# Feed-forward products that read their moving weight columns from last to first and write PSUM in the same reversed order

## The chip, the core and the metric

The kernel runs on one core of one Trainium2 chip. The metric is device time in microseconds (us), the median of several runs. [...]

## The reference, cut to what matters

The reference is one decoder layer on 256 tokens of width 2048, in float32. A mixer (an input projection, three kinds of attention, gated branches, an output projection) is followed by the part that this change touches:

```python
def swiglu(h, w_gate, w_up, w_down):
    return (jax.nn.silu(h @ w_gate) * (h @ w_up)) @ w_down
...
        h = rms_norm(x, norm_ffn[layer])
        x = x + swiglu(h, w_gate[layer], w_up[layer], w_down[layer])
    return rms_norm(x, norm_final)
```

`w_gate` and `w_up` are 2048 x 5632, `w_down` is 5632 x 2048.

## The kernel before

**The products.** Float32 is multiplied in parts. Each factor is split into a high part (type float32r, rounded, called `hi`) and the rest (`lo`), and every product is three matmuls: hi·hi, hi·lo and lo·hi (L638 to L640; L877 to L880 in the up products). Tokens are the stationary operand, a block of 128 features x 128 tokens; weights are the moving operand, 128 features x 256 columns in the feed-forward part. One matmul writes 128 tokens x 256 columns of a PSUM bank (512 float32 columns, so half a bank), and the three matmuls of a product write the same half.

**Units.** The weights come through a ring of four slots in units of 2 x 128 features x 512 columns. For each unit SyncE issues one transfer into `raw_ring`, ScalarE rounds it into `weight_hi_ring` (L1039), VectorE subtracts to get `weight_lo_ring` (L1269), and TensorE uses both: a plain unit is 24 matmuls (2 blocks x 2 token tiles x 2 column halves x 3). The slot is free when the last of them has counted `unit_used` up. The list `FFN` fixes the order of the units: 88 of gate, 88 of up and 88 of down, in two halves of the 5632 columns.

**Two forms of product.** Gate and down units run through `products`. The up units run through `up_unit` and its helper `into`; 55 of the 88 up units do with seven block products instead of eight (21 matmuls, not 24), for which VectorE and ScalarE prepare sums of weights (`weight_sums_hi`, `weight_sums_lo`) and sums of token blocks (`h_sums`). Its other 33 units have 24.

**Where things lie.** The weight rings start 128 bytes into a line of 512 bytes and the stationary tiles 192 bytes into one (`MOVING, STATIONARY = 128, 192`). Each row of 256 moving columns is 1024 bytes without a gap, read upwards.

**After the products.** VectorE and ScalarE read the banks in plain order (silu L1078, up rows L1321 to L1325, the residual add L1348), and TensorE transposes the 512 new columns of activations (L627) for the down products. After the last down unit comes a final norm and the store.

Of the kernel before, what the change touches and what calls it, by code (L numbers as in the profile page):

```python
# [21 lines left out]
TT = 2  # L22
# [3 lines left out]
W = 512  # L26
# [26 lines left out]
UK = 2  # L53
RING = 4
UPC = KD // UK
# [5 lines left out]
Q4 = W // 2  # L61
# [169 lines left out]
def build_layer(nc, x_in, norm_mix, w_in, sinks, pe_k, w1_k, w2_k, pe_v, w1_v, w2_v,  # L231
                w_br_a, w_br_b, w_br_c, w_out, norm_ffn, w_gate, w_up, w_down, norm_final, out):
    ctx = ExitStack()
    with ctx:
# [3 lines left out]
        def at(name, shape, offset, dt=F32):  # L238
            return nc.alloc_sbuf_tensor_at(name, [P] + shape, dt, offset=offset)

        def place(name, shape, dt=F32):
            n = 4
            for s in shape:
                n *= s
            n = (n + 31) // 32 * 32
            t = at(name, shape, top[0], dt)
            top[0] += n
            assert top[0] <= nc.sbuf_top, name
            return t

        raw = place("raw_ring", [RING, UK, W])
        whi = place("weight_hi_ring", [RING, UK, W], F32R)
        wlo = place("weight_lo_ring", [RING, UK, W], F32R)
# [46 lines left out]
        h2T_hi = at("h2T_hi", [KD, S], mid, F32R)  # L300
        h2T_lo = at("h2T_lo", [KD, S], mid + 4 * KD * S, F32R)
        span = [low]

        def follow_on(name, shape, dt=F32):
            n = 4
            for d in shape:
                n *= d
            t = at(name, shape, span[0], dt)
            span[0] += n
            assert span[0] <= mid, name  # L310
            return t

        actT_hi = follow_on("actT_hi", [KH, S], F32R)
        actT_lo = follow_on("actT_lo", [KH, S], F32R)
# [9 lines left out]
        ext_hi = at("weight_sums_hi", [2, 3, Q4], ext_at, F32R)  # L324
        ext_lo = at("weight_sums_lo", [2, 3, Q4], ext_at + 2 * 3 * 4 * Q4, F32R)
# [28 lines left out]
        bank = [ctx.enter_context(nc.psum_tensor(f"bank{i}", [P, W], F32)) for i in range(8)]  # L354

        def sem(name):
            return ctx.enter_context(nc.semaphore(name))
# [4 lines left out]
        unit_used = sem("unit_used")  # L362
# [262 lines left out]
        def _(pe):  # L625
            def transpose(dst, src, n=P):
                return pe.transpose(dst, src, ident[0:n, 0:n])  # L627

            def products(slot, lhs, pair, first, last, k0, width=W, tiles=tuple(range(TT))):

                l_hi, l_lo = lhs
                parts = [(0, Q4), (Q4, W)] if width == W else [(0, width)]
                for k, t, (a, b) in [(k, t, part) for k in range(UK) for t in tiles for part in parts]:
                    dst = bank[2 * pair + t][:, a:b]
                    x_hi, x_lo = (m[:, k0 + k, t * P:(t + 1) * P] for m in (l_hi, l_lo))
                    w_hi, w_lo = (m[:, slot, k, a:b] for m in (whi, wlo))
                    opening = first and k == 0 and a == 0
                    pe.matmul(dst, x_hi, w_hi, start=opening, stop=False, skip_group_check=True)  # L638
                    pe.matmul(dst, x_hi, w_lo, start=False, stop=False, skip_group_check=True)  # L639
                    m = pe.matmul(dst, x_lo, w_hi, start=False, stop=last and k == UK - 1, skip_group_check=True)  # L640
                return m
# [230 lines left out]
            def into(i, b, q, lhs, rhs, stop):  # L872

                l_hi, l_lo = lhs
                r_hi, r_lo = rhs
                dst = bank[b][:, q * Q4:(q + 1) * Q4]
                pe.matmul(dst, l_hi, r_hi, start=(i, b) not in opened, stop=False, skip_group_check=True)  # L877
                opened.add((i, b))
                pe.matmul(dst, l_hi, r_lo, start=False, stop=False, skip_group_check=True)  # L879
                return pe.matmul(dst, l_lo, r_hi, start=False, stop=stop, skip_group_check=True)  # L880

            def quarters(u, k, c):

                return tuple(m[:, u % RING, k, c * Q4:(c + 1) * Q4] for m in (whi, wlo))

            def up_unit(u, i, j):

                def block(k, t):
                    return tuple(m[:, UK * j + k, t * P:(t + 1) * P] for m in (h2T_hi, h2T_lo))

                stop = j == UPC - 1
                if not is_seven(u):
                    for k in range(UK):
                        into(i, 3, 0, block(k, 0), quarters(u, k, 0), stop)
                        into(i, 2, 0, block(k, 0), quarters(u, k, 1), stop)
                        into(i, 2, 1, block(k, 1), quarters(u, k, 0), stop)
                        m = into(i, 3, 1, block(k, 1), quarters(u, k, 1), stop)
                    return m
                n, e = SEVEN.index(j), N_SEVEN[u] % 2
                if i == 0:  # L900
                    pe.wait_ge(h_sum_lo, n + 1)

                def total(r):
                    return tuple(m[:, n, r, :] for m in (h2S_hi, h2S_lo))

                def extra(r):
                    return tuple(m[:, e, r, :] for m in (ext_hi, ext_lo))

                into(i, 6, 0, block(0, 0), quarters(u, 0, 0), True)
                into(i, 3, 0, block(1, 0), quarters(u, 1, 0), False)  # L910
                into(i, 2, 0, total(3), quarters(u, 1, 1), False)
                into(i, 6, 1, total(1), quarters(u, 0, 1), True)
                into(i, 7, 0, total(0), extra(0), True)
                into(i, 7, 1, total(2), extra(1), True)
                return into(i, 2, 1, block(1, 1), extra(2), False)

            def ffn_unit(u):

                what, i, j = FFN[u - U_FFN]
                if what == "gate":  # L920
                    if j == 0 and i == 0:
                        pair_free(Q_FFN)
                    elif j == 0 and half_of(i) != half_of(i - 1):
                        pe.wait_ge(added, TT * (NC_D - 1))
                    elif j == 0:
                        pe.wait_ge(silu_ready, i)
                    if i == 0:
                        pe.wait_ge(t_lo, 2 * UPC + j + 1)
                    pe.wait_ge(lo_ready, u + 1)
                    products(u % RING, (h2T_hi, h2T_lo), 0, j == 0, j == UPC - 1, UK * j).then_inc(unit_used, 1)  # L930
                elif what == "up":
                    if j == 0 and i == 0:
                        pair_free(Q_FFN + 1)
                        pe.wait_ge(squares, 2 * TT * NC_D)
                    elif j == 0:
                        pe.wait_ge(up_emptied, i)
                        if half_of(i) != half_of(i - 1):
                            pe.wait_ge(added, TT * NC_D)
                    pe.wait_ge(lo_ready, u + 1)
                    up_unit(u, i, j).then_inc(unit_used, 1)  # L940
                else:
                    h, c = i
                    n, done = KD_H[h], TT * (NC_D * h + c - 1)
                    if j == 0 and c == 0:
                        pe.wait_ge(silu_ready, HALVES[h][1])
                    elif j == 0 and c == 1:
                        pe.wait_ge(up_emptied, HALVES[h][1])
                    elif j == 0:
                        pe.wait_ge(added, done)
                    if c == 0:  # L950
                        pe.wait_ge(aT_lo, 2 * (HALVES[h][0] + j // 2 + 1))
                    if i == LAST_DOWN and j >= n - RING:
                        return
                    pe.wait_ge(lo_ready, u + 1)
                    products(u % RING, (actT_hi, actT_lo), c % 2, j == 0, j == n - 1, UK * j).then_inc(unit_used, 1)

            def last_units():

                n = KD_H[1]
                for t in range(TT):  # L960
                    for j in range(n - RING, n):
                        u = AT["down", LAST_DOWN, j]
                        if t == 0:
                            pe.wait_ge(lo_ready, u + 1)
                        m = products(u % RING, (actT_hi, actT_lo), LAST_DOWN[1] % 2, False, j == n - 1, UK * j,
                                     tiles=(t,))
                        if t == TT - 1:
                            m.then_inc(unit_used, 1)
                    if t == 0:
                        m.then_inc(tile0_full, 1)  # L970
# [21 lines left out]
            for u in range(UPC):  # L992
# [3 lines left out]
                if u == 3:  # L996
                    pe.wait_ge(rows_ready, 48)
                    pe.wait_ge(gains_ready, 1)
                    for a in range(1, 4):
                        m = transpose(bank[2][:, KD * a:KD * (a + 1)], rows[0:KD, a, :], KD)  # L1000
# [674 lines left out]
```

## Time and profile before

| | |
|---|---|
| median of 3 runs | 1381.56 us (1380.27 to 1384.85) |
| span of the profiled execution, first to last instruction | 1378.3 us |
| TensorE busy | 1364.8 us, 99% of the span |
| TensorE weight loads busy | 1332.1 us, 97% |
| VectorE busy | 922.5 us, 67% |
| ScalarE busy | 702.5 us, 51% |
| mean granted TensorE clock | 0.999 |
| transfers | 261.08 MB, mean 189 GB/s |

The span is of one profiled execution; of its own total time the profile gives only this span, so everything outside it is taken from the distance to the median, 3.3 us. "Busy" of TensorE is the union of matmuls that overlap one another in the pipeline: a single one lasts some 0.28 us from its start to its modelled end, yet another starts every 0.11 us. Its rate is therefore read from the starts, or from how many matmuls a stretch of known length holds.

### The profile page before, as it was taken

The page shows a single profiled execution, that of the slowest core. Times are in us where ns is not written, and L with a number is a line of the kernel's source. Part 1 is how long each engine was busy: PE and PEld are TensorE (multiplying, and loading weights), DVE is VectorE, ACT ScalarE, POOL GpSimd, SP SyncE. Part 2 cuts the span into 40 slices and gives each one's busy share as a digit, 9 for nine tenths or more (in the row PEclk, how much of TensorE's full clock was granted, in tenths as well). Part 3 has the DMA queues.
Part 4 walks back from the last instruction along what each step waited for, and adds up shares of the span by engine and source line. Part 5 has one row for each costly group of instructions (what it writes and reads, how often), then busy time and mean ns, then how long its engine had stood idle before and what let it go on. Part 6 is the DMA issues. An engine that isn't in the chain of part 4 may idle for free.

```text
span 1378.3 us, 26427 instructions
## 1 busy us (share of the span) xinstructions
PE 1364.8 (99%) x11280; PEld 1332.1 (97%) x11280; DVE 922.5 (67%) x1189; ACT 702.5 (51%) x912; POOL 46.2 (3%) x70
## 2 busy tenths in 40 slices
PE   8999999999999999999999999999999999999997
PEld 8999999999999999999999999999999999999997
DVE  6455557667654657666788788875446788887554
ACT  7333356656545654465654555454334455545444
POOL 4000010000000110000000000000000000000111
PEclk9999999999999999999999999999999999999999
DMA  7777755455565767546556756566556665666653
GB/s 255 245 217 217 212 148 154 140 151 141 152 192 163 198 204 221 179 163 200 165 181 198 219 171 196 185 208 210 195 195 181 191 211 172 196 194 231 210 195 123
DMA packets 135264, 261.08 MB, mean 189 GB/s; under 512 B 8448, under 2 KB 25408, under 8 KB 134768
## 3 DMA queue, kind: packets, MB, share of 16 engines
q1 hardware_dynamic: 133328, 251.89, 59.8%
q0 software_dynamic: 1792, 7.57, 1.5%
q8 instruction: 86, 1.41, 0.4%
q14 instruction: 26, 0.21, 0.0%
q10 hardware_dynamic: 32, 0.01, 0.0%
HBM read 257.33 MB, written 2.10 MB: 188 GB/s over the span
## 4 chain that ended last, share of the span: by engine, by line
PE 89%; DVE 8%; ACT 1%; issue 1%; ACTq 0%; POOL 0%; DVEq 0%; POOLq 0%
PE bank L638 24%; PE bank L639 23%; PE bank L640 23%; PE bank L877 5%; PE bank L880 4%; PE bank L879 4%; PE bank L627 2%; DVE weight_lo_ring L1269 2%; DVE weight_sums_lo L1289 1%; DVE weight_sums L1278 1%; PE bank L776 1%; DVE act_rows L1329 1%; ACT weight_hi_ring L1039 1%; PE bank L687 1%; DVE raw_ring L1280 1%
## 5 line engine op out<-in xcount | busy, mean ns | idle before, releaser
L1269 DVE TENSOR_TENSOR weight_lo_ring<-raw_ring,weight_hi_ring 128x1024 fp32r<-128x1024 f32 (+2 forms) x480 | 581.0, 1220 | 317.0 <-ACT weight_hi_ring L1039 263.4
L1039 ACT ACTIVATE weight_hi_ring<-raw_ring 128x1024 fp32r<-128x1024 f32 (+2 forms) x432 | 449.1, 1052 | 348.6 <-PE bank L640 281.1
L638 PE MATMUL bank<-weight_hi_ring,hT_hi 128*128 128x256 f32 (+2 forms) x1280 | 384.5, 300 | 0.8 <-DVE weight_lo_ring L1269 0.8
L639 PE MATMUL bank<-weight_lo_ring,hT_hi 128*128 128x256 f32 (+2 forms) x1280 | 378.0, 295 | 0.0
L640 PE MATMUL bank<-weight_hi_ring,hT_lo 128*128 128x256 f32 (+2 forms) x1280 | 377.8, 295 | 0.0
L638 PEld LDWEIGHTS bank<-weight_hi_ring,hT_hi 128*128 128x128 f32 x1280 | 241.1, 188 | 12.5 <-issue 7.5
L639 PEld LDWEIGHTS bank<-weight_lo_ring,hT_hi 128*128 128x128 f32 x1280 | 240.5, 188 | 4.5
L640 PEld LDWEIGHTS bank<-weight_hi_ring,hT_lo 128*128 128x128 f32 x1280 | 240.4, 188 | 4.7
L638 PE MATMUL bank<-weight_hi_ring,h2T_hi 128*128 128x256 f32 x704 | 196.3, 279 | 2.2 <-DVE weight_lo_ring L1269 2.1
L640 PE MATMUL bank<-weight_hi_ring,h2T_lo 128*128 128x256 f32 x704 | 195.3, 277 | 0.0
L639 PE MATMUL bank<-weight_lo_ring,h2T_hi 128*128 128x256 f32 x704 | 195.2, 277 | 0.0
L638 PE MATMUL bank<-weight_hi_ring,actT_hi 128*128 128x256 f32 x704 | 194.5, 276 | 0.0
L639 PE MATMUL bank<-weight_lo_ring,actT_hi 128*128 128x256 f32 x704 | 194.3, 276 | 0.0
L640 PE MATMUL bank<-weight_hi_ring,actT_lo 128*128 128x256 f32 x704 | 194.3, 276 | 0.0
L638 PEld LDWEIGHTS bank<-weight_hi_ring,h2T_hi 128*128 128x128 f32 x704 | 132.2, 188 | 4.0 <-DVE weight_lo_ring L1269 3.3
L640 PEld LDWEIGHTS bank<-weight_hi_ring,h2T_lo 128*128 128x128 f32 x704 | 132.5, 188 | 0.0
L639 PEld LDWEIGHTS bank<-weight_lo_ring,h2T_hi 128*128 128x128 f32 x704 | 132.5, 188 | 0.0
L639 PEld LDWEIGHTS bank<-weight_lo_ring,actT_hi 128*128 128x128 f32 x704 | 132.2, 188 | 0.0
L638 PEld LDWEIGHTS bank<-weight_hi_ring,actT_hi 128*128 128x128 f32 x704 | 132.2, 188 | 0.0
L640 PEld LDWEIGHTS bank<-weight_hi_ring,actT_lo 128*128 128x128 f32 x704 | 132.2, 188 | 0.0
L1036 ACT ACTIVATE weight_sums_hi<-weight_sums 128x768 fp32r<-128x768 f32 x55 | 46.6, 847 | 127.8 <-DVE weight_sums L1281 61.4
L877 PE MATMUL bank<-weight_hi_ring,h2T_hi 128*128 128x256 f32 x374 | 105.1, 281 | 0.0
(238 smaller groups left out, 1883.2 us busy)
## 6 DMA issues: line engine op xcount, KB each, us to landing
raw_ring<-in_w_in SPq DMA_DIRECT2D x96, 512.0 KB, 3.6
raw_ring<-in_w_gate SPq DMA_DIRECT2D x88, 512.0 KB, 4.3
raw_ring<-in_w_up SPq DMA_DIRECT2D x88, 512.0 KB, 4.2
raw_ring<-in_w_down SPq DMA_DIRECT2D x88, 512.0 KB, 4.1
raw_ring<-in_w_in SPq DMA_DIRECT2D x56, 452.0 KB, 3.7
raw_ring<-in_w_out SPq DMA_DIRECT2D x32, 512.0 KB, 3.9
raw_ring<-in_w_br_c SPq DMA_DIRECT2D x16, 256.0 KB, 3.9
raw_ring<-in_w_br_a SPq DMA_DIRECT2D x16, 256.0 KB, 6.7
```

The source lines that it names most:

```text
L627: return pe.transpose(dst, src, ident[0:n, 0:n])
L638: pe.matmul(dst, x_hi, w_hi, start=opening, stop=False, skip_group_check=True)
L639: pe.matmul(dst, x_hi, w_lo, start=False, stop=False, skip_group_check=True)
L640: m = pe.matmul(dst, x_lo, w_hi, start=False, stop=last and k == UK - 1, skip_group_check=True)
L687: pe.matmul(dst[:, S:2 * S], v[0], pT[:, i % 2, h, 0:S], start=True, stop=False)
L776: m = pe.matmul(bank[4 + h][:, P * t:P * (2 * t + 1)], qT[half, pr, P * t:P * (t + 1)], keys[half, 0:P * (t + 1)], start=True, stop=True)
L877: pe.matmul(dst, l_hi, r_hi, start=(i, b) not in opened, stop=False, skip_group_check=True)
L879: pe.matmul(dst, l_hi, r_lo, start=False, stop=False, skip_group_check=True)
L880: return pe.matmul(dst, l_lo, r_hi, start=False, stop=stop, skip_group_check=True)
L1036: act.activation(ext_hi[:, n % 2, :, :], t_sum[:, :, :], ACT.Copy)
L1039: act.activation(whi[:, s, :, 0:width(u)], raw[:, s, :, 0:width(u)], ACT.Copy).then_inc(hi_ready, 1)
L1269: dve.tensor_tensor(lo, w, hi.bitcast(F32), ALU.subtract).then_inc(lo_ready, 1)
```

## The change

In the feed-forward part each matmul's moving operand is read from its last column to its first, and its PSUM output is addressed from the last column to the first as well. The numbers land where they did before. Addresses of the tiles, the order of the instructions, their count (10383 rows on TensorE in both programs), the waits and the transfers stay the same, as do the products of the mixer, the stationary operands, the transposes and everything that VectorE and ScalarE do.

```diff
-            def products(slot, lhs, pair, first, last, k0, width=W, tiles=tuple(range(TT))):
+            def products(slot, lhs, pair, first, last, k0, width=W, tiles=tuple(range(TT)), back=False):
...
                     dst = bank[2 * pair + t][:, a:b]
+                    if back:
+                        dst = dst[:, ::-1]
                     x_hi, x_lo = (m[:, k0 + k, t * P:(t + 1) * P] for m in (l_hi, l_lo))
                     w_hi, w_lo = (m[:, slot, k, a:b] for m in (whi, wlo))
+                    if back:
+                        w_hi, w_lo = w_hi[:, ::-1], w_lo[:, ::-1]
...
-                dst = bank[b][:, q * Q4:(q + 1) * Q4]
+                dst = bank[b][:, q * Q4:(q + 1) * Q4][:, ::-1]
...
-                return tuple(m[:, u % RING, k, c * Q4:(c + 1) * Q4] for m in (whi, wlo))
+                return tuple(m[:, u % RING, k, c * Q4:(c + 1) * Q4][:, ::-1] for m in (whi, wlo))
...
-                    return tuple(m[:, e, r, :] for m in (ext_hi, ext_lo))
+                    return tuple(m[:, e, r, ::-1] for m in (ext_hi, ext_lo))
```

The gate call, the down call and the one for the last four down units (`last_units`) each get `back=True`. The mixer's calls of `products` don't.

## Rows read from the trace of the kernel before

**Rows 1.** The page: span, and busy time of each engine.
```profile
span 1378.3 us, 26427 instructions
PE 1364.8 (99%) x11280; PEld 1332.1 (97%) x11280; DVE 922.5 (67%) x1189; ACT 702.5 (51%) x912; POOL 46.2 (3%) x70
```

**Rows 2.** The page: granted clock, tenths of full speed, in 40 slices.
```profile
PEclk9999999999999999999999999999999999999999
```

**Rows 3.** The page: the chain that ended last, shares by engine.
```profile
PE 89%; DVE 8%; ACT 1%; issue 1%; ACTq 0%; POOL 0%; DVEq 0%; POOLq 0%
```

**Rows 4.** TensorE's groups, shapes apart: busy us, mean ns of one.
```profile
L638 PE MATMUL bank<-weight_hi_ring,h2T_hi 128*128 128x256 f32 x704 | 196.3, 279 | 2.2 <-DVE weight_lo_ring L1269 2.1
...
L638 PE MATMUL bank<-weight_hi_ring,actT_hi 128*128 128x256 f32 x704 | 194.5, 276 | 0.0
...
L877 PE MATMUL bank<-weight_hi_ring,h2T_hi 128*128 128x256 f32 x374 | 105.1, 281 | 0.0
...
L877 PE MATMUL bank<-weight_hi_ring,h_sums_hi 128*128 128x256 f32 x110 | 30.5, 277 | 0.0
...
L877 PE MATMUL bank<-weight_sums_hi,h_sums_hi 128*128 128x256 f32 x110 | 30.5, 277 | 0.0
...
L877 PE MATMUL bank<-weight_sums_hi,h2T_hi 128*128 128x256 f32 x55 | 15.2, 277 | 0.0
```

**Rows 5.** TensorE in three stretches: length, busy, matmuls, clock, DMA.
```profile
680.00:740.00 60.00, 60.00 (x512) 1.00 0.66 198
...
940.00:1080.00 140.00, 140.00 (x1238) 1.00 0.60 192
40.00:140.00 100.00, 100.00 (x486) 1.00 0.74 223
```

**Rows 6.** TensorE in order of time, in a down chunk.
```profile
939.74 0.28 PE L640 MATMUL bank<-weight_hi_ring,actT_lo 128*128 128x256 f32 x1
939.85 0.28 PE L638 MATMUL bank<-weight_hi_ring,actT_hi 128*128 128x256 f32 x1
939.97 0.28 PE L639 MATMUL bank<-weight_lo_ring,actT_hi 128*128 128x256 f32 x1
940.08 0.28 PE L640 MATMUL bank<-weight_hi_ring,actT_lo 128*128 128x256 f32 x1
```

**Rows 7.** TensorE in order of time, the 452-column products of the mixer.
```profile
99.68 0.37 PE L640 MATMUL bank<-weight_hi_ring,hT_lo 128*128 128x452 f32 x1
```

**Rows 8.** The chain by time: start, us, what; eight passes each.
```profile
318.03 1.73 PE bank L802 x8
...
547.72 0.87 PE bank L627 x8
```

**Rows 9.** TensorE in order of time, a read with a step of two.
```profile
172.97 0.69 PE L725 MATMUL bank<-identity,proj 128*64 128x64 f32 x16
173.59 0.39 PE L638 MATMUL bank<-weight_hi_ring,hT_hi 128*128 128x256 f32 x1
```

**Rows 10.** All engines, the feed-forward stretch: busy and instructions of each.
```profile
660.00:1378.00 718.00, 708.31 (x6187) 705.89 (x6185) 516.73 (x617) 352.48 (x402) 11.14 (x7) 1.00 0.61 192
```

**Rows 11.** Waits of TensorE and VectorE, 655 to 1371: total, times, longest.
```profile
PE bank L638 <- DVE weight_lo_ring L1269: 2.1, 8, 0.6
...
DVE weight_lo_ring L1269 <- ACT weight_hi_ring L1039: 126.8, 93, 2.0
```

**Rows 12.** Groups, shapes apart: the 256-column float32 passes, the transposes.
```profile
L802 PE MATMUL bank<-probs_T,vc_block_diagonal 128*128 128x256 f32 x8 | 1.9, 378 | 0.0
...
L627 PE MATMUL bank<-identity,act_rows 128*128 128x128 f32 x88 | 11.4, 272 | 0.0
```

More of the change, by code:

```diff
@@ L929, in ffn_unit @@
                     pe.wait_ge(lo_ready, u + 1)
-                    products(u % RING, (h2T_hi, h2T_lo), 0, j == 0, j == UPC - 1, UK * j).then_inc(unit_used, 1)
+                    products(u % RING, (h2T_hi, h2T_lo), 0, j == 0, j == UPC - 1, UK * j, back=True).then_inc(unit_used, 1)
                 elif what == "up":
@@ L954, in ffn_unit @@
                     pe.wait_ge(lo_ready, u + 1)
-                    products(u % RING, (actT_hi, actT_lo), c % 2, j == 0, j == n - 1, UK * j).then_inc(unit_used, 1)
+                    products(u % RING, (actT_hi, actT_lo), c % 2, j == 0, j == n - 1, UK * j,
+                             back=True).then_inc(unit_used, 1)
             def last_units():
@@ L965, in last_units @@
                         m = products(u % RING, (actT_hi, actT_lo), LAST_DOWN[1] % 2, False, j == n - 1, UK * j,
-                                     tiles=(t,))
+                                     tiles=(t,), back=True)
                         if t == TT - 1:
```

## The prediction, made before the changed kernel had run

> **What bounds the kernel now.** [...] From 660 to 1378 us it is busy 708.3 of 718.0 us, VectorE 516.7, ScalarE 352.5, DMA 61% [rows 10]. Its waits name only 2.1 us on VectorE's low parts, in 8 places. VectorE does wait, for ScalarE, 126.8 us in 93 places [rows 11], but this is time that it has to spare. So TensorE's own rate sets the end.
>
> That rate comes from how close together the matmuls start. In a down chunk they start at 939.74, 939.85, 939.97, 940.08 [rows 6], 0.113 us apart. A long stretch gives it more exactly: 140 us hold 1238 matmuls [rows 5]; one lasts 277 ns [rows 4], so those that began up to 0.277 us before the stretch are counted too: (140 + 0.277)/1238 = 113.3 ns. [...]
>
> **The change part by part.** How many matmuls: gate and down, each 704 on three lines, are 6 x 704 = 4224. The up products are three lines each of 374, 110, 110 and 55, which is 3 x 649 = 1947 [rows 4]. Together 6171. At 113.3 ns they are 699 us, just over half of the span. Each ns per matmul is worth 6.2 us, or 0.45% of the whole. This is the lever, and nothing hides it.
>
> Nothing else moves. No instruction is added, removed or reordered; transfers, waits, the stationary reads, the 88 transposes [rows 12] and the banks' readers see the same addresses. An edit that leaves TensorE's rate alone is thus free without needing any cover, and one that slows it has none. If it gets slower, the others have more room: VectorE's waits [rows 11] grow, and nothing new is late. If it gets faster, VectorE at 516.7 of 718 us [rows 10] stays below it on average.
>
> The unknown price is that of reading 256 float32r columns downwards and of writing them downwards. No row shows a step of minus one, so I bound it. From below: transposes pass 128 columns in 0.87/8 us = 109 ns [rows 8]. [...]
>
> [...] I take no change: 113.3 ns.
>
> [...]
>
> The sum: 1378.3 us + 6171 x 0 = 1378.3 us of span, and with the 3.3 us between this span and the median, 1381.6 us. I keep 1381.6.
>
> **The rivals.**
> First, half rate. [...] Then 6171 x (216 - 113.3) = 634 us are added, 2015 us. [...] Chance 0.20. [...]
>
> Second, a worse meeting of streams. The same matmul runs at 113.3 or 117.7 ns in stretches that differ in nothing that its own operands show [rows 5], so the rate depends on how the moving stream and the next weight load (97% busy, [rows 1]) fall together. Reversing one and not the other changes it. With all matmuls at 117.7 ns: 6171 x 4.4 = +27 us, less about 3 us for some 90 us which are already there, +24, 1406 us. With 122 ns, no head start: 6171 x 8.6 = +53, 1435 us. Chance 0.18.
>
> Third, a better meeting, by the same argument. [...] At 109 ns: 6171 x 4.3 = -27 us, 1355 us; half of it, 1368. [...] Against it: the offsets 128 and 192 are part of how the streams meet now, and with the other direction nothing says that they'd meet better. Chance 0.17.
>
> That the change does nothing, because hardware or compiler sees the two reversals cancel, gives the same 1381.6 and belongs to my forecast. Chance of that and of a harmless reversal together: 0.45.
>
> **How the numbers follow.** The prediction is that of the likeliest case, 1381.6 us. Alone its range is 1377.5 to 1385.7, that is 0.3%, about what a measurement of this kernel can tell from no change (the three runs lie 0.3% apart). The better meeting reaches down to 1355 and the worse one up to 1435; half rate, with 2 in 10, stays outside. Range 1354 to 1436. Faster by over 0.3%: 0.17. Within: 0.45. Slower: 0.18 + 0.20 = 0.38.
>
> **What would show it.** The down chunk shows it best, since nothing else runs on TensorE in it: 1238 matmuls in 140 us if I am right, some 1191 at 117.7 ns, 650 at 216 ns, 1287 at 109 ns. The mixer's 452-column stretch must hold 486 in 100 us in any case, and the feed-forward part must begin within 1 us of where it does now. If it is half rate, VectorE's waits for ScalarE and for TensorE's banks grow by hundreds of us and DMA falls to a third of the time. If the time changes while the starts stay 113.3 ns apart, my argument is wrong altogether, since then the cost lies in a wait that I don't see. [...]

## The result and the profile after

The changed kernel takes 1399.83 us (median of 4 runs, 1398.67 to 1400.41). The kernel before, beside it, takes 1381.92 us (1380.27 to 1384.85). The ratio is 1.0121, 95% interval [1.0098, 1.0143]. It is slower, by 18 us. I had given "no change" as the likeliest and 0.18 to a worse meeting of streams at 117.7 ns and 1406 us, and that is near what came.

The page of the kernel after: span, busy time of each engine, granted clock, and the shares of the chain that ended last.

```profile
span 1397.8 us, 26427 instructions
...
PE 1387.0 (99%) x11280; PEld 1356.1 (97%) x11280; DVE 922.4 (66%) x1189; ACT 702.8 (50%) x912; POOL 45.4 (3%) x70
...
PEclk9999999999999999999999999999999999999999
...
PE 99%; DMA 0%; DVE 0%; ACT 0%; SPq 0%; ACTq 0%; issue 0%
```

Clock and instruction counts are those of [rows 1, 2]. TensorE has 22 us more of busy time, VectorE and ScalarE have the same as before. The chain had 8% on VectorE in [rows 3] and has none now; 99% of it lie on TensorE.

TensorE in stretches of the kernel after: length, busy, matmuls, clock, DMA. Beside [rows 5] they tell nearly everything.

```profile
680.00:740.00 60.00, 60.00 (x507) 1.00 0.64 193
940.00:1080.00 140.00, 140.00 (x1191) 1.00 0.58 185
...
40.00:140.00 100.00, 100.00 (x486) 1.00 0.73 222
```

The down chunk holds 1191 matmuls where it held 1238: (140 + 0.277)/1191 = 117.8 ns. The mixer's 452-column stretch, which the change doesn't touch, still holds 486. In order of time, in the same down chunk as [rows 6]:

```profile
939.87 0.28 PE L644 MATMUL bank<-weight_hi_ring,actT_lo 128*128 128x256 f32 x1
939.99 0.28 PE L642 MATMUL bank<-weight_hi_ring,actT_hi 128*128 128x256 f32 x1
940.11 0.28 PE L643 MATMUL bank<-weight_lo_ring,actT_hi 128*128 128x256 f32 x1
940.22 0.28 PE L644 MATMUL bank<-weight_hi_ring,actT_lo 128*128 128x256 f32 x1
940.34 0.28 PE L642 MATMUL bank<-weight_hi_ring,actT_hi 128*128 128x256 f32 x1
```

The steps aren't equal any more. In nanoseconds the starts come 115, 118 or 119, and 120 apart, again and again (sum 353.3 ns for three matmuls), where the kernel before has 113 to 114 each time. TensorE runs in a fixed rhythm, and in a slower one. The stretch from 680 us shows yet another rhythm: 507 matmuls are 118.9 ns on average, because from 672 to 712 us the starts lie 120.0 apart and later 117.8. TensorE in its two parts:

```profile
680.00:712.00 32.00, 32.00 (x269) 1.00 0.65 198
714.00:755.00 41.00, 41.00 (x351) 1.00 0.66 204
```

**The account.** From the first to the last feed-forward matmul the trace of before has 719.8 us, that of after 738.8, +18.9. Both traces have the same instructions in the same order, so each distance between two starts can be set beside its counterpart. 6224 of them are under 150 ns in both: 708.4 us before and 732.0 after, +23.6. The other 42, where TensorE of the kernel before waits or passes to or from transposes, have 11.4 us before and 6.8 after, -4.7; 23 of them are under 150 ns now. So the slower pace costs 23.6 us, and 4.7 come back, because TensorE now reaches the places later at which it used to wait for VectorE (2.1 us in 8 places before [rows 11], none after). Most of this lies at the ends of the up chunks: before, a product starts at 807.94 us and the next only at 808.43, on a `weight_lo_ring` that VectorE finished late. After, no such gap follows that up chunk.

### The profile page after: what moved, and what is told of

Read it like the earlier page. It is cut to its first block, busy times and chain, and to the rows that moved or that the text cites. A ratio compares the mean times of both kernels' runs of the same rounds, so it can differ in the third digit from the quotient of the medians.

```text
span 1397.8 us, 26427 instructions
## 1 busy us (share of the span) xinstructions
PE 1387.0 (99%) x11280; PEld 1356.1 (97%) x11280; DVE 922.4 (66%) x1189; ACT 702.8 (50%) x912; POOL 45.4 (3%) x70
## 4 chain that ended last, share of the span: by engine, by line
PE 99%; DMA 0%; DVE 0%; ACT 0%; SPq 0%; ACTq 0%; issue 0%
PE bank L642 26%; PE bank L644 26%; PE bank L643 26%; PE bank L884 5%; PE bank L881 5%; PE bank L883 5%; PE bank L627 2%; PE bank L780 1%; PE bank L691 1%; DMA x<-in_x 0%; PE bank L740 0%; PE bank L692 0%; PE bank L828 0%; PE bank L820 0%; PE bank L806 0%; PE bank L834 0%
## 5 line engine op out<-in xcount | busy, mean ns | idle before, releaser
L642 PEld LDWEIGHTS bank<-weight_hi_ring,hT_hi 128*128 128x128 f32 x1280 | 241.3, 189 | 11.4 <-issue 6.5
L644 PE MATMUL bank<-weight_hi_ring,actT_lo 128*128 128x256 f32 x704 | 198.5, 282 | 0.0
L644 PE MATMUL bank<-weight_hi_ring,h2T_lo 128*128 128x256 f32 x704 | 198.4, 282 | 0.0
L642 PE MATMUL bank<-weight_hi_ring,actT_hi 128*128 128x256 f32 x704 | 197.7, 281 | 0.0
L643 PE MATMUL bank<-weight_lo_ring,actT_hi 128*128 128x256 f32 x704 | 197.4, 280 | 0.0
```

## The experiments

In the expectations "theory 1" is that the downward moving read costs the time, "theory 2" that the downward PSUM write does. Each group of runs had the kernel before beside it. Its medians were 1388.4 us (e1, e2), 1386.2 (o1 to o3), 1383.8 (o4), 1385.5 (o5) and 1382.4 (o6).

### Which of the two reversals

e1 reads backwards and writes upwards:

```diff
-                    if back:
-                        dst = dst[:, ::-1]
...
-                dst = bank[b][:, q * Q4:(q + 1) * Q4][:, ::-1]
+                dst = bank[b][:, q * Q4:(q + 1) * Q4]
```

> The moving columns of the feed-forward products are read from last to first, PSUM is written upwards; the output's columns therefore come out in another order within each half bank. If the cost sits in the moving read (theory 1: the downward moving read meets the next weight load worse), the time is that of the changed kernel, about 1400 us, and 140 us of the down chunk hold some 1191 matmuls (117.8 ns from start to start). If it sits in the downward PSUM write (theory 2), the time is about 1382 us and the same 140 us hold some 1238 (113.3 ns).

e2 writes backwards and reads upwards:

```diff
-                    if back:
-                        w_hi, w_lo = w_hi[:, ::-1], w_lo[:, ::-1]
...
-                return tuple(m[:, u % RING, k, c * Q4:(c + 1) * Q4][:, ::-1] for m in (whi, wlo))
+                return tuple(m[:, u % RING, k, c * Q4:(c + 1) * Q4] for m in (whi, wlo))
...
-                    return tuple(m[:, e, r, ::-1] for m in (ext_hi, ext_lo))
+                    return tuple(m[:, e, r, :] for m in (ext_hi, ext_lo))
```

> The moving columns are read upwards as before, PSUM is written from last column to first, so the columns come out in another order within each half bank. Theory 1 (the moving read) expects about 1382 us and 113.3 ns from start to start, theory 2 (the PSUM write) about 1400 us and 117.8 ns. If both streams contribute, both single reversals lie between 1382 and 1400 us.

Measured: e1 1400.04 us, ratio 1.0103 [1.0076, 1.0131]; e2 1387.41 us, ratio 0.9993 [0.9967, 1.0019]. TensorE in the stretches of e1, read backwards:

```profile
680.00:740.00 60.00, 60.00 (x507) 1.00 0.63 193
940.00:1080.00 140.00, 140.00 (x1191) 1.00 0.58 185
```

And of e2, written backwards:

```profile
680.00:740.00 60.00, 59.77 (x526) 1.00 0.65 202
940.00:1080.00 140.00, 140.00 (x1237) 1.00 0.60 190
```

The read alone gives the changed kernel, to the matmul; the write alone gives the one before. Theory 2 is out. A PSUM bank written from last column to first costs nothing here: 1237 matmuls in 140 us of the down chunk against 1238, and a ratio of 0.9993.

### Is it direction, or how two streams meet? A table of blocks

m1 is a kernel of its own, in which TensorE runs the pattern of a unit (hi·hi, hi·lo, lo·hi over two blocks, two token tiles and two halves) with offsets and directions from a list:

```
CONFIGS: (moving offset, stationary offset, columns, read back, write back)
(128, 192, 256, False, False), (128, 192, 256, False, True), (128, 192, 256, True, False), (128, 192, 256, True, True), ...
```

> Not the layer: one kernel that only runs blocks of the same float32r matmuls on TensorE (48 of 256 columns per block, four transposes between blocks), and computes none of the reference. Blocks: four combinations of read and write direction at the offsets of the layer kernel (moving 128, stationary 192 bytes into a line of 512), each twice; then all 64 pairs of offsets in steps of 64 bytes upwards, and the same 64 downwards; then 128, 256, 384, 452 and 512 columns in both directions. If the pace depends on how the moving read and the weight load meet, it changes with the pair of offsets, differently for the two directions: 113.3 ns at 128/192 upwards, 117.8 ns downwards, and among the 64 downward pairs some are at 113.3 or below. If direction has a price of its own, all 64 downward pairs are at 117.8 ns or above. If offsets play no part, each direction has one pace throughout.

The pace of a block is the mean distance between its starts once the first are left out, in which it settles: eight here, ten in m2, eleven in m3 and m4, three in the blocks of twelve of m3. With another number left out most means move by some tenths of a ns. In ns, for some pairs of offsets (moving/stationary):

| offsets | upwards | downwards |
|---|---|---|
| 128/192 (4 blocks each) | 113.3 in all | 120.0 in 3, 117.8 in 1 |
| 0/0 | 120.0 | 118.4 |
| 0/64 | 113.3 | 120.0 |
| 64/64 | 120.0 | 118.4 |
| all 64 pairs | 113.3 to 120.0 | 118.2 to 120.1 |

So offsets count in both directions, but only upward blocks reach 113.3 ns. At the 16 pairs whose two offsets are equal modulo 256 bytes downward is the faster one (118.2 to 118.4 ns against 120.0). Downwards everything repeats after 256 bytes; upwards it does for all but 8 of the 64 pairs, of which 4 have 113.3 or 117.8 ns where their partners have the other. It is the relation of the two operands that counts: in m1 and m2, whose offsets go in steps of 64 and 32 bytes, every upward block at 113.3 has offsets that differ by 64 modulo 128, and none of the 320 upward blocks with another difference gets below 116.4. (At offsets of odd 16 bytes, in m3 and m4, this no longer holds: 48/192 reaches 113.3.) Widths are the other surprise. TensorE in m1, two stretches with 452 columns (up, down) and two with 512 (up, down):

```profile
875.00:879.00 4.00, 4.00 (x21) 1.00 0.00 0
908.20:912.20 4.00, 4.00 (x21) 1.00 0.00 0
880.50:885.00 4.50, 4.50 (x21) 1.00 0.00 0
914.00:918.50 4.50, 4.50 (x21) 1.00 0.00 0
```

The same number fits either way: the blocks give 206.7 and 206.8 ns, 233.5 and 233.2.

### Does the start of a block decide?

The four blocks that read up and write down or the reverse had 117.8 ns (both that only wrote downwards, and one that only read downwards) or 120.0, although e2, which only writes downwards, shows 113.3 in the layer. So one pair of offsets may have more than one rhythm. m2 starts each block at other moments, and narrows the stationary operand.

> Again only blocks of float32r matmuls, none of the layer (24 of 256 columns per block, after four transposes and, in some blocks, one float32 matmul of 16 to 128 columns that shifts the moment at which the block starts). 64 pairs of offsets in steps of 32 bytes upwards and 16 downwards, six starts each; then stationary blocks of 128, 96, 64 and 32 columns in both directions; then only one or two of the three matmuls of a product read downwards. If the pace comes from how the moving read and the weight load meet, the same pair can settle at 113.3 or 117.8 ns depending on the start when read upwards, no start brings a downward pair to 113.3, and with a weight load of 32 columns both directions have the same pace, nearer to 109 ns. If the downward read itself is slow, 32 columns leave the two directions as far apart as 128.

Upwards at 128/192: nine blocks, six at 113.3 and three at 117.8. Every upward pair of m2 that reached 113.3 also had blocks at 117.8, by the start alone. The upward slow rhythm isn't the downward one: its steps are 117 to 119 ns, not 115, 118 and 120, though three of them sum to the same 353.3. Downwards at 128/192: nine blocks, 117.5 to 117.8 in eight, 120.0 in one; no downward block of any pair is below 117.5. With only one or two of a product's three matmuls read downwards it was 117.6 to 117.9, in 18 blocks of 18: one reversed read takes the fast rhythm from all three. My expectation on narrow stationary blocks failed: with 32 columns the trace has 108 ns for a weight load in place of 188, and downwards the pace was still 118.2 to 118.5, upwards 113.4, 116.5 and 113.4. The rhythm isn't made by the length of the weight load alone.

The layer shows the two upward rhythms too. In the kernel before the starts lie 117.8 ns apart from 650.4 us on, 113.3 after the transposes at 659.6, 117.8 again after a wait at 667.8, and 113.3 from the transposes at 757.4 to the end, apart from some 3 us after each later wait. Each change comes at an interruption, though not every interruption brings one. TensorE in the kernel before, ahead of the change at 757.4 us and behind it:

```profile
714.00:756.00 42.00, 42.00 (x359) 1.00 0.62 190
770.00:806.00 36.00, 36.00 (x320) 1.00 0.66 204
```

### Do the offsets work in the layer too?

o1 is the kernel before, o2 the changed kernel, both with `MOVING, STATIONARY = 0, 0`; o3 is the changed kernel with `0, 64`.

> The kernel before with both offsets at 0 (rings and stationary tiles each begin a line of 512 bytes). The table has 120.0 ns for this pair upwards. If its blocks carry over to the layer, 9819 matmuls of 256 columns (feed-forward and mixer) cost 6.7 ns more each, +66 us: about 1448 us. If placement is nothing in the layer, 1382 to 1390.

> The changed kernel with both offsets at 0. The table has 118.4 ns downwards and 120.0 upwards for this pair. If the cost of reversing is a matter of the meeting, its sign turns here: the feed-forward part is faster than that of the upward kernel with the same offsets by 6171 x 1.6 ns = 10 us, about 1438 us. If reading downwards has a price of its own, it is again some 18 us slower than that kernel.

> The changed kernel with offsets 0 and 64. Table: upwards 113.3 (as at 128/192), downwards 120.0 in place of 117.8 to 120. The mixer keeps its pace, and the feed-forward part has 120.0 ns in the down chunk: 6171 x 2.2 ns more than the changed kernel, about 1413 us. If the offsets don't matter for downward reads, 1400.

Measured: o1 1431.64 us, ratio 1.0332 [1.0306, 1.0359]; o2 1421.44 us, 1.0260 [1.0233, 1.0286]; o3 1400.06 us, 1.0100 [1.0075, 1.0126]. The down chunk of o1, read upwards:

```profile
940.00:1080.00 140.00, 140.00 (x1170) 1.00 0.56 187
```

The down chunk of o2, read downwards:

```profile
940.00:1080.00 140.00, 140.00 (x1186) 1.00 0.58 189
```

1170 matmuls are 119.9 ns, 1186 are 118.3; the table said 120.0 and 118.4. With these offsets the reversed kernel is the faster one, by 10.2 us, as expected to the microsecond. So there is no fixed price of reading downwards: its sign turns with placement. The absolute times I had 17 us too high: 6.7 ns per matmul was counted against 113.3, but the mixer's 256-column matmuls average 114.4 ns in the kernel before, some 90 us of its feed-forward part run at 117.8, and the waits shrank by 5 us. o3 refutes one entry: its down chunk has 1191 matmuls, 117.8 ns, not the 120.0 of the first table. m2 had five of six starts near 117.8 for this pair, so the first table's single block was the rarer rhythm.

### Widths, load length, and a shift of the low parts

> Blocks of float32r matmuls only, none of the layer. Three questions. (1) Widths of 128 to 512 columns in both directions: the first table had the same pace up and down at 384, 452 and 512 columns, so I expect that direction costs something only around 256 columns, where one weight load per matmul is just hidden. (2) Stationary blocks of 64 and 32 columns at eight moving offsets: if the meeting is with the weight load, the offset matters less the shorter the load, and with 32 columns the pace is nearly flat over the offsets in both directions; if the moving read collides with something of its own, it depends on the offset as before. (3) The low parts of the moving or of the stationary operand start 32 to 224 bytes later than the high parts: if two successive moving reads collide, the first shift changes the pace and the second doesn't; if moving read and weight load collide, both do. Lastly odd 16-byte offsets.

In ns at 128/192, three starts each:

| columns | upwards | downwards |
|---|---|---|
| 128 to 224 | 111.5 to 111.8 | 111.7 to 111.8 |
| 256 | 113.3, 117.8, 113.3 | 117.8 |
| 288 | 133.0 to 133.4 | 131.6 |
| 320, 352 | 146.6 to 146.9, 160.0 | 146.6 to 146.8, 160.0 |
| 384 | 173.4 to 176.6 | 176.0 to 176.4 |
| 416 | 186.6 to 186.8 | 190.0 |
| 448 | 201.9 to 202.5 | 204.4 to 206.6 |
| 480 | 215.4 to 216.4 | 220.0 |
| 512 | 233.2 to 233.4 | 233.2 to 233.4 |

"Only around 256" was too simple: up to 224 columns there is a floor of 111.7 ns which direction doesn't touch, and above it direction is worth -1.8 to +4.6 ns, now one way, now the other. With 64 or 32 stationary columns upward blocks still reach 113.3 at some moving offsets and not at others, and no downward one is below 117.8, so the second of these expectations (flat with a short load) is wrong. Shifting the low moving part by any of seven distances loses 113.3 upwards, and so do six of seven shifts of the low stationary part. By the third expectation that speaks for a meeting of moving read and weight load, but it doesn't rule out that two moving reads meet as well. The one shift that keeps 113.3, in three of three starts, is that of the low stationary part by 128 bytes.

o4 turns the mixer's products too:

```diff
-                m = products(u % RING, lhs, q % 2, j == 0, j == n - 1, UK * j, width)
+                m = products(u % RING, lhs, q % 2, j == 0, j == n - 1, UK * j, width, back=True)
...
-                                 UK * j, WQ).then_inc(unit_used, 1)
+                                 UK * j, WQ, back=True).then_inc(unit_used, 1)
```

> The changed kernel with the mixer's products read and written backwards as well. By the theory that the price hangs on the width: the 452-column stretch keeps 486 matmuls in 100 us, the mixer's 3648 products of 256 columns cost some 3.4 ns more (117.8 in place of their mean of 114.4), +12 us over the changed kernel, some of it absorbed by waits: 1408 to 1413 us. If a downward read costs per column, the 672 products of 452 columns get 1.76 x 4.4 ns each too, +5 us more, and the stretch holds 468.

Measured: 1412.68 us, ratio 1.0206 [1.0165, 1.0246]. TensorE in o4, the down chunk and the 452-column stretch:

```profile
940.00:1080.00 140.00, 140.00 (x1192) 1.00 0.57 185
...
40.00:140.00 100.00, 100.00 (x486) 1.00 0.73 222
```

The 452-column products are read downwards at no cost, and the mixer's of 256 columns go from a mean of 114.4 to 117.9 ns. The first feed-forward matmul starts at 664.1 us in place of 650.9. Price per column is out; the price hangs on the rhythm at this width.

### A placement with one rhythm

m4 gives 16 further starts to the candidates.

> Blocks of upward float32r matmuls, none of the layer: 16 combinations of how much later the low parts of the moving and of the stationary operand start (0 to 192 bytes), eight moving offsets, two starts each; then 16 different starts for each of six pairs of offsets, and 16 for the downward read at 128/192. In the table before, the low stationary part 128 bytes later gave 113.3 ns in 3 of 3 starts, the present placement in 2 of 3. If that placement has only the fast state, all 16 starts give 113.3; if the 3 of 3 were luck, some of them give 117.8, as I expect of the present one. Downward, none of 16 starts is below 117.5.

| moving, stationary, low part later by | direction | pace in ns (blocks) |
|---|---|---|
| 128, 192, 0 (both kernels) | up | 113.3 (6), 117.8 (12) |
| 128, 192, 128 | up | 113.3 (18 of 18) |
| 0, 192, 128 | up | 113.3 (9), 118.8 to 118.9 (9) |
| 192, 192, 128 | up | 118.8 to 119.7 (18) |
| 48, 192, 0 | up | 113.3 (15), 113.8 (1) |
| 208, 192, 0 | up | 113.3 (7), 118.4 to 118.8 (9) |
| 128, 192, 0 | down | 117.8 (15), 120.0 (1) |

TensorE in m4, the start of a block with the low part 128 bytes later. It comes in with steps of 0.12 us and finds the fast rhythm by itself: the last step shown is 0.11, and those behind it are 113 or 114 ns. (At 48/192 it takes ten steps or so; with only the first eight left out its means were 113.3 to 114.7.)

```profile
943.81 0.28 PE L465 MATMUL bank<-moving_lo,stationary_hi 128*128 128x256 f32 x1
943.93 0.28 PE L465 MATMUL bank<-moving_hi,stationary_lo 128*128 128x256 f32 x1
944.05 0.28 PE L465 MATMUL bank<-moving_hi,stationary_hi 128*128 128x256 f32 x1
944.17 0.28 PE L465 MATMUL bank<-moving_lo,stationary_hi 128*128 128x256 f32 x1
944.29 0.28 PE L465 MATMUL bank<-moving_hi,stationary_lo 128*128 128x256 f32 x1
944.41 0.28 PE L465 MATMUL bank<-moving_hi,stationary_hi 128*128 128x256 f32 x1
944.52 0.28 PE L465 MATMUL bank<-moving_lo,stationary_hi 128*128 128x256 f32 x1
```

o5 puts that placement into the kernel before, o6 into the changed one. `LO = 128` is added ahead of the five low stationary tiles (`h_sb` and `h_sum` move by as much):

```diff
+        top[0] += LO
         hT_lo = place("hT_lo", [KD, S], F32R)
...
-        h2T_lo = at("h2T_lo", [KD, S], mid + 4 * KD * S, F32R)
+        h2T_lo = at("h2T_lo", [KD, S], mid + 4 * KD * S + LO, F32R)
...
+        span[0] += LO
         actT_lo = follow_on("actT_lo", [KH, S], F32R)
```

> The kernel before (upwards), with the low part of every stationary operand placed 128 bytes further into its line. If this placement has only the fast state, every run lies at about 1378 to 1380 us, since 6171 matmuls keep 113.3 ns and the mixer's 3648 gain some 1 ns each, partly lost in waits; the kernel before scatters from 1380 to 1394. If the single runs of the kernel before scatter for another reason than the two states, this one scatters as much, around 1386.

> The changed kernel (downwards) with the same new placement, low stationary parts 128 bytes further. The table has 118.5, 117.8 and 118.7 ns for it downwards, against 113.3 in 18 of 18 blocks upwards. If the placement helps only where the fast state exists, this kernel gains nothing in the feed-forward part: 739 us from its first to its last matmul (118.5 ns would make it 743), 1391 to 1192 matmuls being ruled out in favour of some 1191 to 1184 in 140 us of the down chunk, and 1396 to 1402 us in all, some 22 us above the upward kernel with the same placement. If the placement cures the downward read too, 1377.

Measured: o5 1376.96 us (1376.19 to 1378.39, 5 runs), ratio 0.9940 [0.9926, 0.9953], faster than both kernels. o6 1400.58 us (1399.90 to 1401.03), ratio 1.0139 [1.0118, 1.0160]. TensorE in o5:

```profile
680.00:740.00 60.00, 59.78 (x526) 1.00 0.68 204
940.00:1080.00 140.00, 140.00 (x1238) 1.00 0.60 190
...
40.00:140.00 100.00, 100.00 (x491) 1.00 0.74 227
```

TensorE in o6:

```profile
680.00:740.00 60.00, 60.00 (x510) 1.00 0.66 202
940.00:1080.00 140.00, 140.00 (x1184) 1.00 0.58 183
```

In o5 the stretch from 680 us, which held 512 matmuls in [rows 5], holds 526. So it does in e2, with the old placement and another entry. The feed-forward part of o5 is as long as in the trace of before (719.6 us): the fast pace is given back in waits and passages, 15.1 us in 49 long distances against 11.4 in 42. What the profiled run gained lies ahead of it, where 452 columns take (100 + 0.37)/491 = 204.4 ns and no longer 206.5, and the part begins at 646.8 us, not 650.4. o6 has 118.5 ns, as m3's table said (118.5, 117.8, 118.7), and 742.2 us for the part. With this placement reversing costs 23.6 us between the two medians, and 27 if each is taken against the kernel before beside it (8.5 us below, 18.2 above).

## Why the prediction was right and where it was not

**What bounds the kernel** held. TensorE, busy 708.3 of 718.0 us from 660 us on [rows 10], sets the end by its own rate, and the count of 6171 matmuls with 6.2 us per ns was the right lever.

**The step that failed** is "I take no change: 113.3 ns". The trace of after shows 117.8 ns, and 120.0 from 672 to 712 us; e1 shows that the read does it. That reading downwards costs nothing was my estimate, and no row of the kernel before showed it. The read with a step of two [rows 9] couldn't tell: it is another shape, 64 columns, and goes upwards. At 256 columns and these offsets the runs don't bear the estimate out (117.8 ns against 113.3); at 512 they do (233.2 to 233.4 either way).

The stated range held all the same, but only because the rivals had widened it. The forecast itself, no change within 0.3%, was missed by 18 us.

**The second rival came true, down to its price per matmul**: with all of them at 117.7 ns it had +24 us, 1406. The pace accounts for 23.6 us, the measured loss is 18 us of median and 19.5 us of span. The term that it put at nothing is the waits. The prediction said that of a slower TensorE nothing new is late, which is so, but it left out that existing waits shrink: -4.7 us. In the price itself there is some luck: 117.7 ns is (60 + 0.277)/512, from 680 to 740 us of the kernel before [rows 5], an upward stretch with steps of 117 to 119 ns, and the downward read has another rhythm that happens to have the same mean. No run says why the two agree.

**Its reason was only half right.** It blamed how the moving stream and the next weight load fall together. That pace depends on the offsets of both operands is shown (m1 to m4, o1, o2), and so is that the same operands have two rhythms. But a weight load of 108 ns in place of 188 leaves the gap between the directions (m2, m3), and shifting one moving part against the other also changes the pace, so successive moving reads may meet each other too. Which unit collides stays open; no run separates the two reads, and the direction of the weight load was not varied.

**Half rate and a better meeting** didn't come: no downward block anywhere took more than 120.2 ns at 256 columns, or less than 117.5. The rivals' sums use three more paces, which no run shows for a 256-column float32r matmul. The 216 ns of half rate is 1.73/8 us, the mixer's float32 passes [rows 8]. The 122 ns "with no head start" is 256 times (206.5 - 113.3)/196 = 0.476 ns, the mean price of a column from 256 to 452, where (100 + 0.37)/486 = 206.5 ns [rows 5, 7]. The 109 ns is the pace of the transposes of 128 columns; the lowest at 256 columns was 113.3 ns in any block, upwards, and even 128 columns took 111.7 (m3).

**What would show it** was chosen well: "some 1191 at 117.7 ns" in the down chunk is the number that the trace has, and the 452-column stretch kept its 486. The feed-forward part begins at 650.9 us, 0.6 later than before, and VectorE's waits for ScalarE grew from 126.8 to 140.1 us, as foreseen.

## What to carry to other kernels

When TensorE is the bound, read the distance between starts, not the busy share, and compare it between stretches of one shape: two paces in one trace of the same work (here 113.3 and 117.8 ns) are a sign that placement or entry decides. In this kernel offsets alone, upwards, gave medians from 1377.0 to 1431.6 us, but only 0.6% of that lies below the kernel before. Before reversing or striding a moving operand, or when moving its tile, measure blocks of that exact width, offsets and direction with several starts each; a single block can show the rarer rhythm, as m1's entry for o3 did. And price a slower bound engine together with the waits that it swallows (here 4.7 us), a faster one with those that it uncovers (in o5 15.1 us against 11.4).

## What the runs showed of the hardware that I had not expected

- Float32r matmuls of 256 columns with a new stationary operand each settle into fixed rhythms, above all 113.3, 117.8, some 118.5 and 120.0 ns. Which one depends on both operands' offsets, on direction, and for some offsets on the moment of entry (m1 to m4). In m1 and m2, in steps of 64 and 32 bytes, 113.3 came only where the two offsets differ by 64 modulo 128.
- At the kernel's own offsets both 113.3 and 117.8 exist upwards, which fits the scatter of the kernel before, 1378 to 1394 us over all its runs. e2, which reads upwards at the same offsets, scatters by 12 us, while kernels for which the blocks show only one of these two (after, e1, o5) scatter by 1.0 to 2.2. That this is the cause is argued from the one profiled run of each, not shown run by run.
- Writing PSUM from the last column to the first costs nothing in the layer: 1237 matmuls in 140 us against 1238, and a ratio of 0.9993 [0.9967, 1.0019].
- From 128 to 224 columns one such matmul follows another after 111.7 ns, in either direction (m3).
